# Gated delta rule on raw keys and queries: score products from the channel-major tiles, norms and decay as scales per token

## The reference

```python
qb = l2_norm(to_heads(q_b, N_HEADS_GDN))      # x * rsqrt(sum(x*x) + 1e-6)
kb = l2_norm(to_heads(k_b, N_HEADS_GDN))
g_log = -exp(a_log) * softplus(a_b + dt_bias)
beta = sigmoid(b_b)

# gated_delta_rule, in chunks; q is scaled by dk ** -0.5
gc = cumsum(g)
decay = exp(where(causal, gc[..., :, None] - gc[..., None, :], -inf))
k_beta = k * beta[..., None]
a_low = where(strict, einsum("bhnid,bhnjd->bhnij", k_beta, k) * decay, 0.0)
t_mat = a_low + eye(L)
rhs = concatenate([v * beta[..., None], k_beta * exp(gc)[..., None]], axis=-1)
u, w = split(triangular_solve(t_mat, rhs, lower=True, unit_diagonal=True))
attn = where(causal, einsum("bhnid,bhnjd->bhnij", q, k) * decay, 0.0)
# per chunk, in order
v_new = u_i - w_i @ state
o = (q_i * exp(g_i)) @ state + a_i @ v_new
state = state * exp(g_last) + (k_i * exp(g_last - g_i)).T @ v_new
# after it
y_b = rms_norm(o, gdn_norm) * silu(z)
```

## Time and profile before

| | |
|---|---|
| median of 3 runs | 969.88 us (969.68 to 971.83) |
| the profiled execution, whole | 969.85 us |
| its span in the profile | 968.0 us |
| mean granted TensorE clock | 0.998 of full speed |
| TensorE busy | 99% of the span |
| GpSimd busy | 77% |
| ScalarE busy | 53% |
| VectorE busy | 38% |
| data moved | 167 MB |

### The profile page before, as it was taken

How to read it: one execution, slowest core, us unless ns; L and a number is a source line. 1 busy time by engine, 2 the same in 40 slices (tenths; PEclk the granted TensorE clock), 3 DMA queues, 4 the chain that set the end, 5 groups by cost and what they waited for, 6 DMA issues and landing times.

```text
span 968.0 us, 14697 instructions
## 1 busy us (share of the span) xinstructions
PE 958.0 (99%) x5708; PEld 815.1 (84%) x5708; DVE 365.8 (38%) x844; ACT 511.5 (53%) x753; POOL 742.8 (77%) x593
## 2 busy tenths in 40 slices
PE   9999999999999999999999999999999999999997
PEld 8988879988878888888888887899888888888885
DVE  5687625785624245031122245052343241111103
ACT  6576635464644347455354556584566564444431
POOL 5967654876654988899877987778876889888890
PEclk9999999999999999999999999999999999999999
DMA  7746242654434766767644665656565557666541
GB/s 261 216 132 196 89 137 77 181 154 149 132 110 137 255 213 179 237 193 211 202 153 139 211 219 168 233 155 187 182 196 152 152 163 228 182 189 192 179 130 44
DMA packets 76750, 167.33 MB, mean 173 GB/s; under 512 B 8348, under 2 KB 13704, under 8 KB 76552
## 3 DMA queue, kind: packets, MB, share of 16 engines
q1 hardware_dynamic: 71296, 156.40, 53.3%
q10 hardware_dynamic: 5384, 9.99, 3.2%
HBM read 165.32 MB, written 1.05 MB: 172 GB/s over the span
## 4 chain that ended last, share of the span: by engine, by line
PE 97%; DVE 1%; ACT 1%; DMA 0%; issue 0%; DVEq 0%; ACTq 0%
PE L L517 23%; PE L L519 22%; PE L L518 22%; PE Q L519 2%; PE Q L517 2%; PE Q L518 2%; PE L L889 2%; PE L L891 2%; PE L L890 2%; PE Q L734 1%; PE Q L1185 1%; PE L L788 1%; PE L L790 1%; PE L L789 1%; PE Q L852 1%; PE L L827 1%
## 5 line engine op out<-in xcount | busy, mean ns | idle before, releaser
L504 POOL TENSOR_TENSOR w_lo<-raw,w_hi 128x512 fp32r<-128x512 f32 x588 | 741.3, 1299 | 201.7 <-ACT w_hi L1333 201.1
L1333 ACT CAST w_hi<-raw 128x1024 fp32r<-128x1024 f32 x294 | 305.2, 1055 | 244.1 <-PE L L519 106.2
L517 PE MATMUL L<-w_hi,uH 128*128 128x512 f32 (+1 forms) x768 | 305.4, 398 | 0.3
L519 PE MATMUL L<-w_hi,uL 128*128 128x512 f32 (+1 forms) x768 | 296.6, 386 | 0.0
L518 PE MATMUL L<-w_lo,uH 128*128 128x512 f32 (+1 forms) x768 | 296.1, 386 | 0.0
L519 PEld LDWEIGHTS L<-w_hi,uL 128*128 128x128 f32 x768 | 144.3, 188 | 29.8
L517 PEld LDWEIGHTS L<-w_hi,uH 128*128 128x128 f32 x768 | 144.5, 188 | 29.3 <-DVE uL L1949 1.5
L518 PEld LDWEIGHTS L<-w_lo,uH 128*128 128x128 f32 x768 | 144.7, 188 | 26.5 <-issue 0.5
L517 PE MATMUL L<-w_hi,hH 128*128 128x512 f32 x176 | 69.0, 392 | 0.0
L519 PE MATMUL L<-w_hi,hL 128*128 128x512 f32 x176 | 68.6, 390 | 0.0
L518 PE MATMUL L<-w_lo,hH 128*128 128x512 f32 x176 | 68.5, 389 | 0.0
(11 more groups left out here) (367 smaller groups left out, 1288.3 us busy)
## 6 DMA issues: line engine op xcount, KB each, us to landing
raw<-in_w_in SPq DMA_DIRECT2D x88, 512.0 KB, 3.7
raw<-in_w_ffn_gate SPq DMA_DIRECT2D x22, 512.0 KB, 3.7
raw<-in_w_ffn_up SPq DMA_DIRECT2D x22, 512.0 KB, 3.6
raw<-in_w_ffn_down SPq DMA_DIRECT2D x22, 512.0 KB, 3.6
raw<-in_w_gate SPq DMA_DIRECT2D x22, 512.0 KB, 3.7
raw<-in_w_up SPq DMA_DIRECT2D x22, 512.0 KB, 3.7
raw<-in_w_down SPq DMA_DIRECT2D x22, 512.0 KB, 3.5
raw<-in_w_out SPq DMA_DIRECT2D x16, 512.0 KB, 3.6
```

What stands on the lines that cost most here:

```text
L504: last = nc.gpsimd.tensor_tensor(lo[:, cc], raw[:, n % RAW, cc], hi[:, cc].bitcast(F32), ALU.subtract)
L517: mm(dst, sH, wH, start=start, stop=False)
L519: return mm(dst, sL, wH, start=False, stop=stop)
L1333: copy(halves[SLOT[u]][0], raw[:, u % RAW, :]).then_inc(w_hi_there, 1)
```

## The change

The scores are formed from the raw channel-major tiles C, as the convolution leaves them. The turning back in `feat` (28 turns per group), its copies, the scaling that fed it and the tiles kT, kbqT, kb and qe are gone. The inverse norms, beta and the decay come in elsewhere, as scales per token: the squared inverse norm times beta (`vshare`) on the scores of keys by keys, on u and on the update's correction (`less`, its negative); the key's norm times its inverse (`kinv`) on the values; the query's inverse norm on the output's own norm (`rq2`, `rq`). The keys for the state (kdec) and for w (kbe) are scaled straight out of the turned banks in `tok`. The decayed queries qeT are C times `rowsE`, a new tile that ScalarE exponentiates out of bank Q[1] in `decay` before VectorE overwrites that bank. ScalarE squares out of the banks and copies only the values. In `scan`, VectorE takes u out of the banks. TensorE's score products move ahead of the third weight unit of `feat`.

The diff, cut to its core:

```diff
@@ build: tiles
-        kT = big("kT", 24, TOKENS)
-        kbqT = big("kbqT", 28, [P, NT, GH, 2, HD])
-        gsb = big("gsb", 24, [P, NT, D])
-        tok = big("tok", 36, [P, NT, 3, GH, HD])
+        gsb = big("gsb", 36, [P, NT, D])
+        vtok = big("vtok", 44, TOKENS)
-        kb = big("kb", 72, TOKENS)
+        rowsE = big("rowsE", 72, [P, GH, HD])
@@ TensorE: conv, tok, feat, scan
-                        if pair == 0 and k == 2 and inside_:
+                        if pair == 0 and k == 3 and inside_:
...
-                                pe.wait_ge(*AC(step, "out", (b - 3) // NT, (b - 3) % NT))
+                                pe.wait_ge(*AC(step, "sq", (b - 3) // NT, (b - 3) % NT))
+                            if b == 5:
+                                pe.wait_ge(*VE(step, "kdec"))
                             elif b == 0:
                                 pe.wait_ge(*VE(("decay", gr), "decay log", 1))
...
-                    for b, (what, t) in enumerate(lots):
-                        if b == 3:
-                            fill(step, 1)
-                        pe.wait_ge(*VE(step, what, t))
-                        if b >= 3:
-                            pe.wait_ge(*AC(step, "out", b - 3))
+                    fill(step, 1)
+                    pe.wait_ge(*AC(("tok", gr), "out", 1))
+                    pe.wait_ge(*VE(("tok", gr), "roots"))
+                    for t in range(NT):
                         for i in range(GH):
-                            last = turn(Q[b % 3][:, i * P:(i + 1) * P], src[what](t, i), ident)
-                        last.then_inc(*PE.mark(step, "turned", b))
-                    fill(step, 2)
...
+                            last = mm(Q[2 * t + i // 2][:, (i % 2) * 256:(i % 2 + 1) * 256], C[:, GH + i, t * P:(t + 1) * P],
+                                      C[:, i:GH + i + 1:GH, t * P:(t + 1) * P], start=True, stop=True)
...
+                    fill(step, 2)
                     fill(step, 3)
...
-                    pe.wait_ge(*AC(step, "u", 0))
+                    pe.wait_ge(*VE(step, "vn", 0))
@@ ScalarE: decay, tok
                     actf(edec, edec, ACT.Exp).then_inc(*AC.mark(step, "edec"))
+                    act.wait_ge(*PE(step, "rows", 1))
+                    actf(rowsE[:], Q[1][:].rearrange("p (h d) -> p h d", h=GH), ACT.Exp).then_inc(*AC.mark(step, "rowsE"))
...
+                    squares(0, 0)
                     fill(("decay", step[1]), 3)
...
                     squares(0, 1)
+                    squares(1, 0)
                     fill(step, 0)
...
                     squares(1, 1)
-                    token_major(2, 0)
+                    values(0)
                     fill(step, 1)
-                    token_major(2, 1)
+                    values(1)
@@ VectorE: tok
+                    sums(0, 0)
+                    sums(0, 1)
+                    dve.wait_ge(*AC(step, "sq", 1, 0))
+                    dve.wait_ge(*AC(("decay", gr), "edec"))
+                    tt(kdec[:], heads(Q[2]), over(edec, HD), ALU.mult, step, "kdec")
+                    sums(1, 0)
+                    dve.wait_ge(*AC(step, "sq", 1, 1))
+                    tt(kbe[:], heads(Q[0]), over(eg[:, GH:2 * GH], HD), ALU.mult)
+                    sums(1, 1)
                     ts(s2, s2P, EPS, None, ALU.add, None)
-                    rsqrt(rqP, s2, bank=Q[3])
...
+                    rsqrt(rq, s2, bank=Q[3])
...
+                    tt(vshare.rearrange(th, t=NT), rqv[:, :, 1, :], rqv[:, :, 1, :], ALU.mult)
+                    tt(vshare.rearrange(th, t=NT), vshare.rearrange(th, t=NT), bet, ALU.mult, step, "roots")
@@ VectorE: decay, feat, within, scan
+                        else:
+                            dve.wait_ge(*AC(step, "rowsE"))
                         tt(heads(Q[t]), heads(Q[t]), over(gcv[:, t, :], P), ALU.subtract)
...
+                    tt(qeT[:], C[:, 0:GH, P:SEQ], rowsE[:], ALU.mult)
+                    for t in range(NT):
+                        dve.wait_ge(*AC(("tok", step[1]), "out", t))
+                        tt(vtok[:, t], vtok[:, t], over(kinv[:, t * GH:(t + 1) * GH], HD), ALU.mult)
...
+                            for i in range(2):
+                                n_ = t * GH + 2 * pair + i
+                                vector_next(V.scalar_tensor_tensor(out=AT[:, t, 2 * pair + i], in0=kk_[:, i, 1, :], scalar=vshare[:, n_:n_ + 1],
+                                                                   in1=Dm[:, t, 2 * pair + i], op0=ALU.mult, op1=ALU.mult))
...
-                    dve.wait_ge(*AC(step, "u", 1))
+                    for t in range(NT):
+                        dve.wait_ge(*PE(step, "u", t))
+                        tt(vn[:, t], heads(Q[t]), over(vshare[:, t * GH:(t + 1) * GH], HD), ALU.mult, *((step, "vn", 0) if t == 0 else ()))
                     dve.wait_ge(*PE(step, "wS"))
-                    tt(vn[:, 1], vn[:, 1], heads(Q[2]), ALU.subtract, step, "vn")
+                    for i in range(GH):
+                        vector_next(V.scalar_tensor_tensor(out=vn[:, 1, i], in0=Q[2][:, i * P:(i + 1) * P], scalar=less[:, i:i + 1],
+                                                           in1=vn[:, 1, i], op0=ALU.mult, op1=ALU.add), *((step, "vn", 1) if i == GH - 1 else ()))
...
-                        ts(rv[:, 0:GH], soP, 1.0 / HD, EPS, ALU.mult, ALU.add)
-                        rsqrt(r1[:, t * GH:(t + 1) * GH], rv[:, 0:GH], bank=Q[3])
+                        tt(rv[:, 0:GH], soP, rq2[:, t * GH:(t + 1) * GH], ALU.mult)
+                        ts(rv[:, 0:GH], rv[:, 0:GH], 1.0 / HD, EPS, ALU.mult, ALU.add)
+                        rt_ = r1[:, t * GH:(t + 1) * GH]
+                        rsqrt(rt_, rv[:, 0:GH], bank=Q[3])
+                        tt(rt_, rt_, rq.rearrange("p (t a h) -> p t a h", t=NT, a=2)[:, t, 0, :], ALU.mult)
```

More of the change, by code:

```diff
@@ L413, in build @@
         rq = tiny(16)
+        rq2, kinv, vshare, less = tiny(8), tiny(8), tiny(8), tiny(4)
         mx, nm, rs, ri = tiny(16), tiny(16), tiny(16), tiny(16)
@@ L925, in last_outputs @@
                 step = ("scan", gr)
-                pe.wait_ge(*VE(step, "vn"))
+                pe.wait_ge(*VE(step, "vn", 1))
                 for i in range(GH):
@@ L1129, in _ @@
                         for i in range(GH):
-                            last = mm(Q[t][:, i * P:(i + 1) * P], TT[:, t, i, :], tok[:, t, 2, i, :], start=True, stop=True)
+                            last = mm(Q[t][:, i * P:(i + 1) * P], TT[:, t, i, :], vtok[:, t, i, :], start=True, stop=True)
                         last.then_inc(*PE.mark(step, "u", t))
@@ L1525, in _, with squares @@
                 elif kind == "tok":
-                    def token_major(part, t):
+                    def squares(part, t):
                         act.wait_ge(*PE(step, "turned", part, t))
[L1528 to L1533, removed]
                         if part > 0:
@@ L1537, in squares, with values @@
                             act.wait_ge(*VE(("scan", 0), "sum", t))
-                        actf(sq[t][:], tok[:, t, part, :, :], ACT.Square).then_inc(*AC.mark(step, "sq", part, t))
-                    token_major(0, 0)
+                        src = Q[(part * NT + t) % 3][:].rearrange("p (h d) -> p h d", h=GH)
+                        actf(sq[t][:], src, ACT.Square).then_inc(*AC.mark(step, "sq", part, t))
+                    def values(t):
+                        act.wait_ge(*PE(step, "turned", 2, t))
+                        copy(vtok[:, t], Q[(2 * NT + t) % 3][:].rearrange("p (h d) -> p h d", h=GH)).then_inc(*AC.mark(step, "out", t))
+                    squares(0, 0)
                     fill(("decay", step[1]), 3)
-                    squares(0, 0)
-                    token_major(0, 1)
-                    token_major(1, 0)
                     squares(0, 1)
+                    squares(1, 0)
                     fill(step, 0)
-                    squares(1, 0)
-                    token_major(1, 1)
                     squares(1, 1)
-                    token_major(2, 0)
+                    values(0)
                     fill(step, 1)
-                    token_major(2, 1)
+                    values(1)
                     fill(step, 2)
@@ L1564, in _ @@
                     gr = step[1]
[L1565 to L1572, removed]
-                    fill(step, 3)
+                    for i in range(4):
+                        fill(step, i)
                 elif kind == "att":
@@ L1626, in _ @@
                 elif kind == "scan":
-                    for t in range(NT):
-                        act.wait_ge(*PE(step, "u", t))
-                        copy(vn[:, t], Q[t][:].rearrange("p (h d) -> p h d", h=GH)).then_inc(*AC.mark(step, "u", t))
                     act.wait_ge(*PE(step, "wT"))
@@ L2111, in _, with sums @@
                     s2v = s2P.rearrange("p (t a h) -> p t a h", t=NT, a=2)
-                    for part in range(2):
-                        for t in range(NT):
```

(21 more changed lines are left out.)

34 lines of the change are left out of this document (10 added, 24 removed).

## The result

The changed kernel took 982.04 us (median of 4 runs, 980.78 to 983.41) against 970.82 for the kernel before on the same chip: ratio 1.0116, 95% interval 1.0096 to 1.0137. It is **slower by 1.2%**; the prediction said 967.0, with 965.2 to 969.2 as its range. The profiled execution took 981.65 us with a span of 979.8, so the span grew by 11.8 us.

The account below looks back on a forecast made before the run. TensorE, busy 958.0 of 968.0 us, was taken as the bound. Turns -6.42, scan -1.11, waits +3.95 (group 0) and +0.54 (group 1), restarts +0.2 gave -2.8 us: 969.85 to 967.0 us, range 965.2 to 969.2.

Parts of the forecast that it names:

- Turns removed: Feature step: 28 TensorE turns fewer per group save 3.21 us each, 6.42 us for both; scores keep their price.
- slower rival: Feature step scores: moving operand in two runs costs more, a doubling (+6.5 us) gives 973.5 us; chance 0.05.
- Decay wait: Decay step, group 0: VectorE waits for rowsE, 2.37 us later; TensorE's first token turns at 67.1, 2.2 us idle.
- kdec wait: Token step: last block of turns waits for kdec, delay 3.95 us in group 0 (first wait included), 0.54 in group 1.
- Scan: Scan, group 0: VectorE takes over ScalarE's copy, TensorE's wait before the state product goes, 1.11 us saved; group 1 nothing.
- What is hidden: Work off TensorE's path costs nothing: VectorE's score products end at about 91, the attention turns come at 94.3.
- The wait behind the second scan: Thinnest cover, 0.2 us left before the output's turns; 0.2 us of wait if four correction instructions pay 0.38 each.
- The clock: Rival: TensorE's clock falls at group 0's two idle stretches, 1.6 us per fall; 968.6 or 970.2 us; chance 0.05.
- the two waits of 2 us: Group 0: two idle stretches of TensorE of about 2.2 us within 9 us, before the first and last token turns.
- the rivals: Whole kernel: waits hidden 962.3 (0.08), 275 ns turns 958.0 (0.02), longer chain 969.0 (0.15), clock falls (0.05), slower operand (0.05).

Follow-up runs that it names:

- e2: Changed kernel with the chain of small per-token scale instructions keeping one operand in bank Q[3]; 967.38 us, ratio 0.9971.
- e3: Changed kernel with VectorE's second-tile difference written into bank Q[2], so VectorE no longer waits for rowsE; 977.64 us, ratio 1.0075.
- e6: Changed kernel with 15 unread TensorE products ahead of the attention turns of each group; 977.26 us, ratio 1.007.
- e1: Changed kernel with GpSimd's low halves cut to 8 columns around the small instructions (output wrong there); 967.46 us, ratio 0.9967.
- e8: Changed kernel with GpSimd's low halves around the token step in instructions of 256 columns instead of 512; 968.14 us, ratio 0.9973.
- e9: Changed kernel with the same GpSimd low halves in instructions of 1024 columns instead of 512; 985.63 us, ratio 1.0148.

## Why the prediction was wrong

- **Turns removed: right.** The scores start at 85.32, behind two weight units; the strided moving operand costs nothing (3.61 us, rows 2 and here). The slower rival by that way falls.
- **Decay wait: right in group 0** (turns at 66.90, forecast 67.1; wait 2.00, forecast 2.2).
- **kdec wait: right.** Turns at 73.94, forecast 74.06. The row shows a wait of only 0.26, because the twelve turns and part of the unit behind the first wait ran at the lower clock, and that time would otherwise have been waited (1.89 in e2, where no fall came). In group 1, 0.36 for the forecast 0.54.
- **Scan: right.** No wait before the state product: it follows w by 0.90 us (157.16 to 158.06), where it was 1.91.
- **What is hidden: this step failed.** TensorE did come to the attention turns at 94.38 (98.90 less 4.52; forecast 94.3). VectorE's last score product ended at 98.76, not at about 91; in e2, with the scales in the bank, it ends at 90.47. The chain has seventeen small instructions (the prediction counted fourteen), and six of them, priced at 0.2 us each, had all their inputs in SBUF: 6.99 us together instead of 1.2, so 5.8 too few. qeT cost 1.73 for 0.69 and vtok 3.34 for 1.4: 3.0 too few. The price came from rows of instructions with one input in a bank, and I took it for every small instruction. The wait behind the second scan came too (0.4 us, where I had left 0.2 of cover): an instruction of 4 columns with all inputs in SBUF takes 1.17 us there, because GpSimd has just started again. In e3 it starts just before GpSimd does, takes 0.16, and there is no wait.
- **The clock:** its rival was weighed for the two waits of 2 us, and had 1.6 us for a fall from the start of the kernel. It fell at the first of these in the changed kernel, where the kdec wait behind it took up what that cost, and in each wait of 4.5 us, at 2.4 us each; none of the rivals had those longer waits. In e2, which has just the waits that were forecast, it stayed up.

The sum as measured: -6.4 turns, -1.1 scan, +3.8 and +0.4 for the forecast waits, +9.0 for the attention turns, +4.8 for the clock there, +0.4 behind the second scan: +10.9 of the 11.8 us. TensorE's starts say where most of the last 0.9 is: these waits are the idle time of the rows, and the work behind one starts a little later still. The attention turns of group 0 start 5.3 us later than before (98.90 against 93.62), which is -3.2 + 3.8 + 4.7, so a wait of 4.5 us delays by almost 4.7; and over the wait of 0.4 us behind the second scan the delay grows by 0.6, from 11.1 (attention scores of group 1, 250.11 against 238.96) to 11.7 (the output's turns, 317.98 against 306.27). That is some 0.5 us for the three waits; the other 0.4 I can't place.

The kernel before had shown it, in rows I didn't read because they lie off the path. Groups by form, VectorE, kernel before:

```profile
L2199 DVE TENSOR_TENSOR Td<-AT,table 64x256 f32<-64x256 f32 x8 | 10.0, 1253 | 0.3
L1910 DVE TENSOR_TENSOR Td<-table,Td 128x512 f32<-128x512 f32 x2 | 3.1, 1574 | 0.2
```

Half the columns and half the partitions of kdec, no input in a bank, and 1253 ns; a full one 1574. Priced by these, the six small instructions come to 7.5 us instead of 1.2 and the three large ones to 4.7 instead of 2.1; VectorE's products end at 91 + 8.9 = 99.9, 5.6 us behind TensorE in each group, and the forecast is 967.0 + 11.2 = 978, on the other side.

The same trace shows the second condition too. VectorE in group 0, kernel before, and GpSimd:

```profile
92.20 0.68 DVE L1910 TENSOR_TENSOR kbe<-kb,small 128x512 f32<-128x512 f32 x1
...
74.62 17.49 POOL L504 TENSOR_TENSOR w_lo<-raw,w_hi 128x512 fp32r<-128x512 f32 x14 [0.53 <-ACT w_hi L1333]
```

Both inputs of kbe are in SBUF, and it takes 0.68 us: GpSimd had stopped at 92.11 and started again at 97.87. So such an instruction has two prices in one trace, and what GpSimd does at its place tells which one holds.

## What to carry to other kernels

An instruction's size is not its price: look for the same *places* of its operands (SBUF or a bank of PSUM, the accumulation memory), in a stretch where the same neighbours run. Before moving a scale from PSUM to SBUF for tidiness, see whether GpSimd is busy there; if it is, keep one operand in a bank, or cut GpSimd's instructions shorter. And treat a long wait of TensorE as costlier than it looks, since the work behind it may run at the lower clock.

## What the runs showed of the hardware

- **VectorE waits until GpSimd's running instruction ends, and GpSimd until VectorE's ends.** With all inputs in SBUF and GpSimd busy: 1.2 us for 4 to 8 columns in an unbroken row (0.17 to 0.19 with GpSimd nearly off), 1.7 for 512 (0.69). With one input in a bank: 0.17 and 0.69 beside the same GpSimd work. The price follows GpSimd's instruction: 0.68, 1.2 and 2.3 us for 0.74, 1.34 and 2.35. One that starts late in GpSimd's instruction pays only the rest: 0.80 for the first of the row, 0.75 for qeT in e2. GpSimd's own instruction takes 1.74 us instead of 1.30 beside VectorE's large ones. The Trainium skill (SBUF — State Buffer, section Who interferes with whom) has a rule for this: a VectorE instruction with two SBUF inputs contends with a GpSimd one that reads SBUF, and the port pair that they share is an exclusive lock. The traces agree with both, by the ends named above. Instructions with one input, in SBUF (TENSOR_SCALAR), paid too, 1.2 us; the same section lets them contend when they run in a 2-port mode. Which mode they ran in no run shows.
- **A wait of 4.5 us lowers TensorE's clock** to its lower level (0.51 and 0.53 granted in the two stretches shown) for about 7 us and costs 2.4 us more; with TensorE kept busy in the wait (e6) the clock stays at 1.00. After the 2.0 us before the first turns it fell in the changed kernel and in e6, and not in e1, e2, e8 and e9, where the same turns start within 0.2 us of the same time (66.89 to 67.05). What decides that stays open.
- **A moving operand in two runs of 128 columns** is as fast as a contiguous one: 3.61 us for sixteen instructions both ways.
